# Forget sums carried as spare rows of queries and keys, earlier first quads, and a new order of the output projection and of the border between layers

## What is computed

```python
h = rms_norm(x, norm1_g[layer])
dq, dk, dv, fq, fk, fv, ff, ga, gb = jnp.split(h @ w_in[layer], split_points, axis=-1)
y_diff = diff_attention(...)             # 4 heads, two softmaxes each, a relative bias
y_fox = forgetting_attention(fq, fk, fv, ff + b_forget[layer])
merged = sigmoid(ga) * (y_diff @ w_diff_o[layer]) + sigmoid(gb) * (y_fox @ w_fox_o[layer])
x = x + merged @ w_out[layer]
x = x + peer_ffn(rms_norm(x, norm2_g[layer]), w_query[layer], sub_keys[layer], expert_u, expert_v)
```

```python
c = cumsum(log_sigmoid(f_logit), axis=1)
logits = q @ k.T * scale + (c[q] - c[k])       # causal, then softmax and values
```

## Time and profile before

| | |
|---|---|
| median of 3 runs | 3355.19 us (3353.67 to 3368.07) |
| profiled execution, own time | 3354.05 us |
| its span | 3352.3 us, 43774 instructions |
| TensorE matmuls busy | 3037.2 us (91%) |
| VectorE busy | 2361.1 us (70%) |
| ScalarE busy | 1015.1 us (30%) |
| DMA over the span | 993.57 MB, 296 GB/s |

### The profile page before, as it was taken

One profiled execution on the slowest core, in us unless ns is written; L12 is line 12 of the kernel. 1 busy time (PEld: TensorE's weight loads), 2 busy tenths in 40 slices (PEclk: granted clock), 3 DMA queues, 4 the chain that ended last, 5 costly groups with the idle time before them and its releaser, 6 DMA issues. The chain is left out here.

```text
span 3352.3 us, 43774 instructions
## 1 busy us (share of the span) xinstructions
PE 3037.2 (91%) x15872; PEld 2422.3 (72%) x15872; DVE 2361.1 (70%) x4777; ACT 1015.1 (30%) x2028; POOL 1292.7 (39%) x1194
## 2 busy tenths in 40 slices
PE   8999899988787889979999799958999999999999
PEld 5877566655544577647667576828997999996898
DVE  6745988876666686499897766676654787856564
ACT  2312322210231232232121100025545544445543
POOL 1103777777767211166766767670000000000000
PEclk9999999989998999989999899979999999999999
DMA  9647999999999866699999999994561687752352
GB/s 363 218 153 263 377 409 405 404 405 409 389 379 380 313 232 239 248 349 406 408 397 409 395 409 409 409 400 147 182 225 51 232 271 250 262 168 95 112 184 102
DMA packets 273719, 993.57 MB, mean 296 GB/s; under 512 B 31633, under 2 KB 32401, under 8 KB 273249
## 3 DMA queue, kind: packets, MB, share of 16 engines
q0 software_dynamic: 170960, 625.89, 48.4%
q1 hardware_dynamic: 100960, 361.15, 30.0%
q10 hardware_dynamic: 1584, 3.75, 0.3%
HBM read 989.61 MB, written 1.05 MB: 296 GB/s over the span
## 5 line engine op out<-in xcount | busy, mean ns | idle before, releaser
L285 PE MATMUL bank<-hT,ring 128*128 128x256 f32 x3744 | 844.0, 384 | 11.2 <-ACT hT L915 9.6
L285 PEld LDWEIGHTS bank<-hT,ring 128*128 128x128 f32 x3744 | 719.2, 193 | 143.2 <-issue 35.8
L411 POOL DMA_INDIRECT gring<-in_expert_u,idx x512 | 601.1, 1174 | 340.0 <-issue 145.7
L411 POOL DMA_INDIRECT gring<-in_expert_v,idx x512 | 603.2, 1178 | 290.8 <-DVE pre L1354 142.2
L580 PE MATMUL bank<-gring,dg 128*128 128x512 f32 x1012 | 538.3, 679 | 178.9 <-DMA gring<-in_expert_v,idx 168.6
L1354 DVE CUSTOM_DVE_ANT_0 gring<-gring,t_tok 128x1024 f32<-128x1024 f32 x512 | 603.1, 1224 | 25.3 <-DMA gring<-in_expert_u,idx 23.6
L580 PEld LDWEIGHTS bank<-gring,dg 128*128 128x128 f32 x1012 | 212.5, 217 | 444.0 <-issue 402.8
L1659 DVE TENSOR_TENSOR wl<-ring,wr 128x1024 fp32r<-128x1024 f32 x309 | 377.9, 1224 | 220.4 <-ACT wr L1654 220.0
L1325 DVE SCALAR_TENSOR_TENSOR x<-gring,wts,x 128x1024 f32<-128x1024 f32 x259 | 332.9, 1285 | 261.8 <-DMA gring<-in_expert_v,idx 230.0
L1663 PE MATMUL bank<-hr,wr 128*128 128x258 f32 (+1 forms) x1512 | 430.6, 285 | 1.5 <-DVE hl L2125 0.7
L1665 PE MATMUL bank<-hr,wl 128*128 128x258 f32 (+1 forms) x1512 | 427.2, 283 | 0.0
(11 more groups left out here) (328 smaller groups left out, 3910.0 us busy)
## 6 DMA issues: line engine op xcount, KB each, us to landing
ring<-in_stream SPq DMA_DIRECT2D x679, 512.0 KB, 4.9
t_tok<-in_ada POOLq DMA_DIRECT2D x56, 512.0 KB, 4.9
gring<-in_ada POOLq DMA_DIRECT2D x56, 512.0 KB, 5.0
lat_ada<-in_ada POOLq DMA_DIRECT2D x48, 512.0 KB, 5.1
gring<-in_expert_u,idx POOLq DMA_INDIRECT x512, 11.4
gring<-in_expert_v,idx POOLq DMA_INDIRECT x512, 11.0
na_bias_sb<-in_na_bias POOLq DMA_DIRECT2D x1, 4096.0 KB, 15.4
x<-in_x SPq DMA_DIRECT2D x2, 512.0 KB, 4.1
```

Source lines behind the costliest of these rows:

```text
L285: last = pe.matmul(out, w[:, k * P:(k + 1) * P], act_T[:, k, :], start=(k == 0), stop=(k == KD - 1))
L411: pool.indirect_dma_start(out=gring[:, N % GR, :], out_offset=None, in_=table, in_offset=bass.IndirectOffsetOnAxis(ap=idx[:, b, 4 * (Q % 3 ...
```

## The change

- `pick` and its two matmuls per head go. A head's queries and keys lie on 64 of 128 partitions; the running sum c is now written into row 64 (even heads) or row 0 (odd heads) of the queries, with -1 in the next row, and 1 and c into the same rows of the keys. So the keys are copied out twice by ScalarE (`fox_k`), and four DMAs a layer on ScalarE's queue write the c rows (after job 3's and job 7's filler). Job 8's logits come after its two fillers.
- Four modulation products leave the stretch ahead of the forget gate (8 + 2L becomes 4 + 2L); one each goes to n = 16 and 17, the rest beside the merge.
- Output projection of block 1: one unit, transposes, one unit, two query halves, scores of head 0, the other six units. Then query half, transposes of block 1, query half, scores of head 1.
- GpSimd's wait for the last output unit goes to the first gather into the merged tokens' place: the 11th of layer 0 as before, the third of layer 1.
- The first head's routing exponential goes ahead of the query loop, the weights of quads 0 to 4 to h = 1, 2, 4, 5, 7 and the sums of quads 0 to 3 to h = 2, 4, 6, 7.
- Border: the transposes go ahead of quad 62's sums, a dummy GELU loads its table behind the square root, and layer 1's first splits of second-block weights go ahead of the quad.

```diff
@@ -41,6 +41,10 @@
 EARLY_HEADS = 2
+WEIGHTS_AT, SUM_AT = {1: 0, 2: 1, 4: 2, 5: 3, 7: 4}, {2: 0, 4: 1, 6: 2, 7: 3}
+CROW = (HD, 0)
 LAT, CTX = 0, 1
@@ -394,7 +399,7 @@
                         pool.wait_ge(idx_ready, 16 * L + route_at(b, h) + 1)
-                    if n == 10:
+                    if n < GR and (8 * QUADS * L + n) % GR == 10:
                         pool.wait_ge(unit_done, used(f"ou{L}", 7))
@@ -452,6 +457,11 @@
+        def fox_k(hp, m):
+            return 2 * hp if m else 20 + hp
         def pe_filler(pe, L, f):
@@ -478,14 +488,10 @@
                 pe.wait_ge(pj_ev, 32 * L + 12 + hp + 1)
-                pe.wait_ge(cT_ev, L + 1)
-                pick = one["pick"]
+                pe.wait_ge(c_rows, 64 * (L + 1))
                 for m in range(2):
-                    out, h = bank[J % 2][:, m * nk:(m + 1) * nk], 2 * hp + m
-                    pe.matmul(out, qkT[:, 8 + h, b * P:(b + 1) * P], qkT[:, 20 + hp, 0:nk], start=True, stop=False)
-                    pe.matmul(out, cT[:, b * P:(b + 1) * P], pick[:, h:h + 1].to_broadcast([NH, nk]), start=False, stop=False)
-                    last = pe.matmul(out, pick[:, NH + h:NH + h + 1].to_broadcast([NH, P]), cT[:, 0:nk],
-                                     start=False, stop=True)
+                    last = pe.matmul(bank[J % 2][:, m * nk:(m + 1) * nk], qkT[:, 8 + 2 * hp + m, b * P:(b + 1) * P],
+                                     qkT[:, fox_k(hp, m), 0:nk], start=True, stop=True)
             last.then_inc(a_lg, 1)
@@ -751,10 +757,13 @@
                     if n < 16:
-                        pe_logits1(pe, L, n)
+                        if n != 8:
+                            pe_logits1(pe, L, n)
                         for _ in range(1 if n < 8 or n >= 14 else 2):
...
                             f += 1
+                        if n == 8:
+                            pe_logits1(pe, L, n)
                     else:
@@ -789,18 +798,18 @@
                 pe_out(pe, L, 0, range(KD))
-                pe_out(pe, L, 1, range(4))
+                pe_out(pe, L, 1, range(1))
                 pe_transposes(pe, z + 1, 0)
-                pe_out(pe, L, 1, range(4, 6))
+                pe_out(pe, L, 1, range(1, 2))
                 pe_normed(pe, z + 1, 0)
...
                     pe_query_half(pe, L, t, 0)
-                pe_out(pe, L, 1, range(6, KD))
                 pe_scores(pe, L, 0, 0)
-                for t in range(2, 2 * EARLY_HEADS):
-                    pe_query_half(pe, L, t, 0)
+                pe_out(pe, L, 1, range(2, KD))
+                pe_query_half(pe, L, 2, 0)
+                pe_transposes(pe, z + 1, 1)
+                pe_query_half(pe, L, 3, 0)
                 pe_scores(pe, L, 1, 0)
-                pe_transposes(pe, z + 1, 1)
                 pe_normed(pe, z + 1, 1)
@@ -812,8 +821,8 @@
                                 pe_scores(pe, L, h - 1, b)
-                    if h >= 4:
-                        pe_sum(pe, L, h - 4)
+                    if h in SUM_AT:
+                        pe_sum(pe, L, SUM_AT[h])
                 for b in range(NB):
@@ -822,9 +831,9 @@
                         next(steps, None)
-                    pe_sum(pe, L, Q - 1)
                     if Q == QUADS - 1:
                         pe_transposes(pe, z + 2, 0)
+                    pe_sum(pe, L, Q - 1)
                     for _ in range(turns[2 * (Q - PEQ) + 1]):
@@ -870,10 +879,16 @@
                 act.wait_ge(unit_done, used(f"fq{L}", f))
-                act_two_heads(act, qkT[:, 8 + 2 * f:10 + 2 * f, :], bk).then_inc(pj_ev, 1)
+                for m in range(2):
+                    last = act.activation(qkT[:, 8 + 2 * f + m, :], bk, ACT.Identity, bias=half[:, 3 + m:4 + m],
+                                          scale=half[:, m:m + 1])
+                last.then_inc(pj_ev, 1)
             elif f < 8:
                 act.wait_ge(unit_done, used(f"fk{L}", f - 4))
-                act.activation(qkT[:, 20 + f - 4, :], bk, ACT.Copy).then_inc(pj_ev, 1)
+                for m in range(2):
+                    last = act.activation(qkT[:, fox_k(f - 4, m), :], bk, ACT.Identity, bias=half[:, 7 + m:8 + m],
+                                          scale=half[:, 5 + m:6 + m])
+                last.then_inc(pj_ev, 1)
             else:
@@ -1062,10 +1077,23 @@
                         nk = (n // 4 % 2 + 1) * P
-                        att_exp(act, JOBS1[L] + n, 2, nk, True)
+                        if n != 8:
+                            att_exp(act, JOBS1[L] + n, 2, nk, True)
                         for _ in range(1 if n < 8 or n >= 14 else 2):
...
                             f += 1
+                        if n == 8:
+                            att_exp(act, JOBS1[L] + n, 2, nk, True)
+                        if n == 3:
+                            act.wait_ge(cT_ev, L + 1)
+                            act.wait_ge(pj_ev, 32 * L + 12)
+                            for m in range(2):
+                                act.dma_start(qkT[CROW[m]:CROW[m] + 1, 8 + m:16:2, :], cT[m:NH:2, :]).then_inc(c_rows, 16)
+                        if n == 7:
+                            act.wait_ge(pj_ev, 32 * L + 16)
+                            for m in range(2):
+                                act.dma_start(qkT[CROW[m] + 1:CROW[m] + 2, fox_k(0, m):fox_k(0, m) + (7 if m else 4):1 + m, :],
+                                              cT[m:NH:2, :]).then_inc(c_rows, 16)
                     else:
@@ -1098,10 +1126,12 @@
                     act.activation(qkT[:, t, 0:P], bank[4 + t % 2][:, 0:P], ACT.Copy).then_inc(wq_half_ev, 1)
+                    if t == 2:
+                        act_norm_evac(act, z + 1, one["norm2_g"][:, L], [1])
                     if t % 2:
                         act_scores(act, L, t // 2, 0)
-                act_norm_evac(act, z + 1, one["norm2_g"][:, L], [1])
                 act_norm_squares(act, z + 1, [1])
+                act_route_exp(act, L, 0, 0)
                 for h in range(PH):
@@ -1110,10 +1140,8 @@
                                 act_scores(act, L, h - 1, b)
-                    if h == 2:
-                        act_route_exp(act, L, 0, 0)
-                    if h >= 3:
-                        act_gather(act, L, h - 3)
+                    if h in WEIGHTS_AT:
+                        act_gather(act, L, WEIGHTS_AT[h])
                 for b in range(NB):
@@ -1121,14 +1149,15 @@
                         next(steps, None)
+                    if L == DEPTH - 1 and QUADS - 3 <= Q < QUADS - 1:
+                        for s in range(2):
+                            act_high(act, 2 * (Q - QUADS + 3) + s)
                     if Q == QUADS - 1:
...
                         act_norm_squares(act, z + 2, [0])
-                    if L == DEPTH - 1 and QUADS - 3 <= Q < QUADS - 1:
-                        for s in range(2):
-                            act_high(act, 2 * (Q - QUADS + 3) + s)
+                        act.activation(stat[:, 0, 12:13], half[:, 2:3], ACT.Gelu)
                     if Q == QUADS - 1:
@@ -1467,7 +1496,7 @@
                     dve.tensor_copy(v_tok[:, b, 0:512], bank[4 + 2 * b][:, :]).then_inc(v_evd, 1)
-                dve_ada(dve, L, 8 + 2 * L)
+                dve_ada(dve, L, 4 + 2 * L)
                 dve.wait_ge(const_in, CONSTS)
@@ -1511,6 +1540,8 @@
                         dve_ada(dve, L, 2)
+                    elif n >= 16:
+                        dve_ada(dve, L, 1)
@@ -1551,11 +1582,11 @@
                                lambda: [next(steps, None) for _ in range(now[1])])
-                    if Q == QUADS - 2:
-                        dve_norm_scale(dve, z + 2, [0])
                     if L == DEPTH - 1 and QUADS - 3 <= Q < QUADS - 1:
...
                             dve_low(dve, 2 * (Q - QUADS + 3) + s)
+                    if Q == QUADS - 2:
+                        dve_norm_scale(dve, z + 2, [0])
                 for _ in steps:
@@ -2311,7 +2342,12 @@
     io["x"] = v["x"][0].reshape(NB, P, D).transpose(1, 0, 2)
-    io["half"] = np.concatenate([np.kron(np.eye(2), np.full((HD, 1), HD ** -0.5)), np.full((P, 1), EPS)], 1).astype(f)
+    half = np.concatenate([np.kron(np.eye(2), np.full((HD, 1), HD ** -0.5)), np.full((P, 1), EPS), np.zeros((P, 6))], 1)
+    for m in range(2):
+        r = CROW[m]
+        half[:, 5 + m] = 1
+        half[r + 1, 3 + m], half[r:r + 2, 5 + m], half[r, 7 + m] = -1, 0, 1
+    io["half"] = half.astype(f)
     io["ident"] = np.eye(P, dtype=f)
```

8 lines of the change are left out of this document (4 added, 4 removed).

## The result

| | before | changed, first measurement | changed, second measurement |
|---|---|---|---|
| median, us | 3355.95 (3353.67 to 3368.07) | 3304.26 (3297.95 to 3309.74) | 3291.09 (3282.37 to 3293.88) |
| ratio to before on the same chip | | 0.9838, 95% interval 0.9809 to 0.9868 | 0.9811, 0.9797 to 0.9824 |
| span of the profiled execution | 3352.3 | 3307.9 | 3289.3 |

In the second measurement before took 3352.31. So the change saves 52 us by the first measurement and 61 by the second; forecast were 68. The readings here are from its profile where nothing else is said; why the first trace differs is told further down.

A forecast was written before the change was run, and what follows sets the result against it. It saw a chain of stages with different limits: TensorE in the attention jobs, DMA bytes in the quads. Terms 13.5 + 31.2 + 18 + 5.5 = 68.2 us off 3354.05 gave 3285.9, forecast 3287, range 3264 to 3312.

The forecast's parts named there:

- the transition gives nothing: Rival: quad stage bound by bytes, earlier gathers only displace weight loads TensorE then waits for; 3305 us, chance 0.13.
- the jobs do not shorten: Rival: VectorE keeps waiting for late TensorE values, only 7 us a layer come off; 3304, or 3318; chance 0.09.
- Start of attention: Up to the first logits: fewer products bring the forget gate forward, TensorE's waits go; 13.5 us for both layers.
- the 1.7 us for layer 1's slow filler: Filler behind layer 1's long forget-gate wait, slowed by the clock after idling, returns to 3.62 us; 1.7 us saved.
- Jobs 8 to 15: Attention jobs: cheaper logits make VectorE the limit, 75.7 us against 91.3; 15.6 us a layer, 31.2 for both.
- Transition: From attention into the query loop and first quads: gathers and loop start earlier; 9 us a layer, 18 for both.
- the lead is the loop's own 8.7: First quads: by quad 4 only the query loop's earlier start remains as lead, rounded to 9 us a layer.
- less standing still: Start of the quad stage: DMA loses some 3 us less by idling, within the 9 us a layer.
- Borders: End of each layer's quads: GELU table load and block's copies leave the path; 5.5 us for both.
- The c rows land late: Rival: the rows' DMAs take 8.4 us plus issue against 7.2 available, delaying job 8; 3297 us, chance 0.06.
- Slower: Rival: ScalarE waits at h = 1 and 2 for dot products, holding up query copies and TensorE; 3373 us, chance 0.03.
- More than counted: Rival: early dot products keep DMA full, 14 us a layer, and jobs nearly reach TensorE's 20; 3268 us, chance 0.14.

The follow-up runs named there:

- control: The changed kernel run again with nothing edited; 3291.09 us, the second measurement.
- n8_old_place: Changed kernel with job 8's logits ahead of its two fillers again; 3304.22 us, ratio 0.9860.
- rank1_back: Changed kernel with forget sums as matmuls again, one key copy, no c-row DMAs, job 8's logits ahead of its fillers; 3318.56 us, ratio 0.9906.
- order_back: Changed kernel with output projection, transposes and query halves in their old order, new places of weights, sums and routing exponential kept; 3305.85 us, ratio 0.9857.
- sooner_5: Changed kernel with weights of quads 0 to 4 at h = 1 to 5 and sums of quads 0 to 3 at h = 2, 3, 5, 6; 3278.00 us.
- quads_sooner: Changed kernel with quad 2's weights at h = 3, quad 4's at h = 6 and quad 2's sum at h = 5; 3273.70 us, ratio 0.9763.

## Why the prediction was right, and where it was off

The forecast was 3287, range 3264 to 3312; the two measurements gave 3304 and 3291. The first lies outside the 3278 to 3296 given for the main case and on the times of two rivals ("the transition gives nothing" at 3305, "the jobs do not shorten" at 3304): from that time alone nothing could be told, and that it fell into the range is owed to the range's width. The stages of the control's trace and the undoing of each part decide it. By them the mechanism held in the start of attention, the jobs, the order of the output projection and the border; it failed for the early weights and sums. The sizes were 5 us too large in sum.

- **Start of attention**, 13.5 forecast, 11.6 measured. The waits went as said. The term that fell is the 1.7 us for layer 1's slow filler: I put its low clock down to the idle time ahead of it. That time is gone and the filler takes 5.86 us, 0.6 more than before; the clock fell already in the 8-column matmuls ahead of it. Layer 0 made up for part of it: its filler, which I had not counted, went from 5.78 to 4.65 us.
- **Jobs 8 to 15**, 31.2 forecast, 29.7 measured. Right in layer 0 to 0.2 us and in its reason: VectorE nearly end to end behind two fillers. Layer 1 is 1.1 longer, where matmuls at the end of the stage ran at the lower clock. The rows were no delay: n8_old_place shows them landing 3.7 us after the start of their issue, as the small row does, and in the control, where the core's DMA moved 250 GB/s between the second issue and job 8's logits, TensorE did not wait for them. The Trainium skill (DMA: Bandwidth & Descriptors, Issuing engines are not separate DMA queues) says that they interleave with the weight stream on the same 16 DMA engines; that this would make them late was my own step, and for 4 KB it did not.
- **Transition**, 18 forecast with the first quads, 15.6 by the trace and 14 by the undoing. The step "the lead is the loop's own 8.7" was right: the first gather comes 9.7 us earlier, and the order alone gives all of it. The step that failed is the 3 us "less standing still", the part of the early weights and sums: undone, they cost nothing (-1.9 us). The waits of VectorE of 8 and 10 us that I had estimated at h = 4 and 7 were 11.4 and 9.9 in layer 0 and 8.0 and 6.8 in layer 1, and in layer 0 DMA idles behind them. That moving those two quads was worth 17 us in both layers, as much as the whole transition gives, I had not priced at all; I had only used the waits to cap the lead. Layer 0 kept 4.9 us and layer 1 10.7, where I had 9 for each: that the sum of both came out within 3 us is in part luck. The longer waits of layer 0 go with its smaller gain; no run isolates that.
- **Borders**, 5.5 forecast, 6.6 by the stage table, 4.7 to 6.4 by the undoing. The size is near. That each border has its half, as forecast, is not shown: behind the last gather the undoing cost 4.0 us in layer 1 and nothing in layer 0. With the drain of the Trainium skill (ScalarE: Activation LUTs, What ACT_TABLE_LOAD costs) beside each load the estimate would have been 8.3; what was measured lies below.
- **Rivals.** "The jobs do not shorten" and "the transition gives nothing" are excluded by rank1_back and order_back. "The c rows land late" is excluded by n8_old_place and by the missing wait in the control. "Slower" needed waits of TensorE for the query copies, and even in sooner_5 none is over 1.48 us. "More than counted" did not happen; quads_sooner comes near its time (3274 for 3268), by an edit that the change did not make.

The range was needed for the first measurement, which lies 17 us over the forecast: 4 of them are the terms above, and the other 13 are what made that measurement differ from the second, the part that stays open.

## What to carry to other kernels

When a wait is removed by moving work up, list the waits of the same engine that come next and price them too: here they took back what the early quads gave, and three table entries changed again were worth as much as the whole reordering of the output projection. Read what is worth what by undoing each part alone: the two parts of the transition were forecast as one term, and one of them was worth nothing. A time inside the range does not show this; here it lay on two rivals' times. And take a second trace before building a theory on waits of 2 to 3 us that have no releaser in the profile.

## What the runs showed of the hardware that I had not expected

- A DMA of 4 KB from SBUF to SBUF on ScalarE's queue was there 3.1 us after its issue ended and 3.7 after it began, in a stretch in which the core's DMA moved 184 GB/s.
- An idle time of 4.77 us on TensorE cost 2.3 us more through the clock: two fillers in 9.35 us instead of 7.07.
- The clock can fall while TensorE is busy: to a mean of 0.91 in 1148 to 1149 us of the control, in 32 matmuls with 8-column operands, with a filler of 5.86 us instead of 3.62 behind them and a wait of 0.42. In layer 0 it stayed at 1.00 through the same matmuls.
- The same kernel took 3304 us in one measurement and 3291 in another, while before differed by 4.
